# A decode step behind every half of the up phases, and one per two chunks in the down phases

## The reference, cut to what matters

```python
def _conv_ffn(x, buf, w_up, b_up, w_conv, b_conv, w_down):     # of the prompt, T = 2048
    h = jnp.einsum('btd,df->btf', x, w_up) + b_up               # D_MODEL 1024 -> 2 * D_FF, D_FF = 2816
    full = jnp.concatenate([buf.astype(h.dtype), h], axis=1)
    hc = b_conv + full[:, 0:T] * w_conv[0]
    for j in range(1, CONV_WIDTH):                              # CONV_WIDTH = 3
        hc = hc + full[:, j:j + T] * w_conv[j]
    gate, val = hc[..., :D_FF], hc[..., D_FF:]
    out = jnp.einsum('btf,fd->btd', jax.nn.gelu(gate) * val, w_down)
    ...
# of the decoded positions: q (8, 8, 8, 64), k_past and v_past (8, 8192, 8, 64) through page_table
s = jnp.einsum('bqhd,bkhd->bhqk', q, k) * ATTN_SCALE
s = s + qc[..., :, None] - kc[..., None, :]
p = jax.nn.softmax(jnp.where(causal, s, NEG_INF), axis=-1)
att = jnp.einsum('bhqk,bkhd->bqhd', p, v)
```

## Time and profile before

| what | value |
|---|---|
| median of three runs | 3660.61 us |
| the profiled execution's own time | 3655.41 us |
| its span | 3653.7 us |
| joint stage, PE's first to last matmul | 1459.8 to 3466.8, 2007 us |
| PE busy, whole span | 3179.5 us (87%) |
| DVE, ACT, POOL busy | 2090.3, 1744.2, 504.3 us |
| mean granted TensorE clock | 0.951 |

### The profile page before, as it was taken

One profiled execution on the slowest core, in us unless ns is written; L12 is line 12 of the kernel. 1 busy time (PEld: TensorE's weight loads), 2 busy tenths in 40 slices (PEclk: granted clock), 3 DMA queues, 4 the chain that ended last, 5 costly groups with the idle time before them and its releaser, 6 DMA issues. The chain is left out here.

```text
span 3653.7 us, 58230 instructions
## 1 busy us (share of the span) xinstructions
PE 3179.5 (87%) x20136; PEld 2513.4 (69%) x20136; DVE 2090.3 (57%) x3602; ACT 1744.2 (48%) x3497; POOL 504.3 (14%) x666
## 2 busy tenths in 40 slices
PE   6999943488888895999989999989999899999858
PEld 5999931377777684767767777667777677776623
DVE  2111155477777443666667666667666676665656
ACT  2111110366666311346645666446666456666445
POOL 0000000000000253001122111122111131112210
PEclk9999976799999997999999999999999999999979
DMA  4333333432320445657777766777666786757565
GB/s 142 111 115 105 114 119 142 116 74 67 81 60 1 136 152 157 208 173 253 258 242 282 266 224 237 270 266 269 216 244 231 263 288 239 252 196 250 199 264 212
DMA packets 313291, 684.44 MB, mean 187 GB/s; under 512 B 40151, under 2 KB 132215, under 8 KB 303999
## 3 DMA queue, kind: packets, MB, share of 16 engines
q1 hardware_dynamic: 264551, 519.21, 42.6%
q0 software_dynamic: 43840, 144.74, 11.4%
q10 hardware_dynamic: 4608, 16.78, 1.1%
HBM read 601.33 MB, written 79.92 MB: 186 GB/s over the span
## 5 line engine op out<-in xcount | busy, mean ns | idle before, releaser
L1705 DVE TENSOR_TENSOR F_w_lo<-F_raw,F_w_hi 128x512 fp32r<-128x512 f32 x704 | 500.0, 714 | 628.1 <-ACT F_w_hi L1601 626.9
L1601 ACT CAST F_w_hi<-F_raw 128x512 fp32r<-128x512 f32 x704 | 429.0, 614 | 438.5 <-DMA F_raw<-w_down 167.7
L1462 PE MATMUL F_ps_u<-F_x_hi,F_w_hi 128*128 128x512 f32 x1408 | 573.7, 407 | 27.9 <-DVE F_x_lo L1711 27.9
L1463 PE MATMUL F_ps_u<-F_x_lo,F_w_hi 128*128 128x512 f32 x1408 | 553.3, 393 | 0.0
L1464 PE MATMUL F_ps_u<-F_x_hi,F_w_lo 128*128 128x512 f32 x1408 | 552.2, 392 | 0.0
L1896 POOL DMA_DIRECT2D F_vin<-cache_v x512 | 280.6, 548 | 1482.9 <-PE F_ps_d L1529 1413.4
L1462 PEld LDWEIGHTS F_ps_u<-F_x_hi,F_w_hi 128*128 128x128 f32 x1408 | 266.7, 189 | 118.9 <-issue 53.3
L1462 PE MATMUL F_ps_y<-F_w_hi,F_g_hi 128*128 128x512 f32 x704 | 294.9, 419 | 57.2 <-DVE F_w_lo L1705 51.1
L1759 DVE STREAM_TRANSPOSE F_kt<-F_kin 128x1024 f32<-128x1024 f32 x256 | 303.7, 1222 | 39.0 <-PE F_ps_t L1518 23.1
L1464 PEld LDWEIGHTS F_ps_u<-F_x_hi,F_w_lo 128*128 128x128 f32 x1408 | 266.5, 189 | 58.0
L1463 PEld LDWEIGHTS F_ps_u<-F_x_lo,F_w_hi 128*128 128x128 f32 x1408 | 266.9, 190 | 48.5
(11 more groups left out here) (290 smaller groups left out, 5891.4 us busy)
## 6 DMA issues: line engine op xcount, KB each, us to landing
F_kin<-cache_k SPq DMA_DIRECT2D x512, 256.0 KB, 4.3
F_vin<-cache_v POOLq DMA_DIRECT2D x512, 256.0 KB, 4.6
F_raw<-w_up_t SPq DMA_DIRECT2D x176, 512.0 KB, 6.1
F_raw<-w_down SPq DMA_DIRECT2D x176, 512.0 KB, 5.7
S_raw<-w_up_t SPq DMA_DIRECT2D x22, 1024.0 KB, 10.3
sc_qk<-A_qk SPq DMA_DIRECT2D x16, 1024.0 KB, 5.7
S_raw<-w_down SPq DMA_DIRECT2D x11, 1024.0 KB, 9.9
A_prow<-w_in SPq DMA_DIRECT2D x8, 1028.0 KB, 4.9
```

The source lines that it names most:

```text
L1462: nc.tensor.matmul(out, a_hi, b_hi, start=first, stop=False)
L1463: nc.tensor.matmul(out, a_hi, b_lo, start=False, stop=False)
L1601: nc.scalar.copy(w_hi[:, q % 4, :], raw[:, unit % RAW, q % 2 * 512:(q % 2 + 1) * 512]).then_inc(hi_done, 1)
L1705: nc.vector.tensor_tensor(w_lo[:, q % 4, :], raw[:, q // 2 % RAW, q % 2 * 512:(q % 2 + 1) * 512], w_hi[:, q % 4, :].bitcast(F32), ALU.subt ...
```

## The change

One line, the rule that picks the halves with a place for a decode step. An up phase now has a place behind each of its 88 halves. A down phase has one at the second half of every second chunk (halves 0.5, 2.5, 4.5 and so on to 42.5), 22 in all. The number of places stays 88 + 22 = 110 for a block. The steps and their order are the same, and so is the work of each; they are dealt out to other halves. The last step comes at q = 677 instead of 685.

```diff
     def has_slot(q):
         i = q % HB
-        return i % 8 != 7 if i < UPH else (i - UPH) % 2 == 1 and (i - UPH) // 2 % 4 != 3
+        return i < UPH or (i - UPH) % 4 == 1
```

## The result

The change makes the kernel slower: 3694.50 us, median of four runs (3685.72 to 3700.56), against 3657.97 for the kernel before (3654.19 to 3662.54). The ratio is 1.0097, 95% interval 1.0073 to 1.0122, or +36.5 us. Forecast were 3649 us, in a range of 3630 to 3670. Rival (b), the QV steps that had filled waits, had 3677: the nearest, and still 17 us short.

A forecast was written before the change was run, and what follows sets the result against it. PE sets the pace and its work stays, so waits and the clock behind them were summed: -10.6 - 10.9 - 5 + 2 + 2 + 11.1 = -11.4 us, from a median of 3660.61 to 3649; range 3630 to 3670.

The forecast's parts named there:

- Rival (b): Down phases: QV at 9.5 and 21.5 had filled waits that other things set; +16.2 us, 3677, chance 0.13.
- Part 3: Down phases of blocks 0 to 2: 13.6 us of other, small waits fall by 5, between 0 and 10.
- Part 2: First sweep's end, halves 21.5 to 25.0 of blocks 0 to 2: 10.9 us less, bounds 0 and -14.
- Part 4: PE's wait near chunk 10 of the down phases, blocks 0 to 2 together: +2 us, between -4 and +8.
- The rest: Up phases of blocks 1 to 3: QV every 3 halves costs nothing while DVE's and ACT's lead lasts.
- waits that just move: Sign of a wrong prediction: the waits at the sweep's end only move instead of going away.
- Part 5: X groups behind sequences 1 and 3 move into up phases: 1 us a group, +2, between 0 and +5.
- Part 1: Sequence 0's steps Q and R, block 0's up phase: fewer waits for turned keys, -10.6 us, between -5 and -14.
- Part 6: Run of T and V at block 3's end of up phase: five waits of 1.94 us, +11.1, between +2.6 and +20.

The follow-up runs named there:

- e1: Changed kernel with its down-phase places shifted so that QV stands at halves 9.5, 21.5 and 41.5 in blocks 0 to 2: 3662.13 us.
- e12: Changed kernel with QV moved from 10.5 to 9.5 in the down phases of blocks 0 to 2, T left at 6.5: 3681.42 us.
- e8: Changed kernel with the last E and QV of its down phases at 39.5 and 41.5 instead of 38.5 and 40.5: 3687.99 us.
- e10: Kernel before, with QV moved from 9.5, 21.5 and 41.5 to 10.5, 22.5 and 40.5 in blocks 0 to 2: 3665.78 us.
- e2: Changed kernel with block 3 alone under the placement rule from before: 3678.97 us.
- e5: Changed kernel with the edits of e1 and e2 together: 3647.74 us.
- e4: Changed kernel with the next input's loads spread, one DMA at each of chunks 4, 6, 8 and 10: 3669.32 us.
- e11: Changed kernel with T moved from 6.5 to 5.5 in the down phases of blocks 0 to 2: 3687.47 us.
- e9: e5 with the X groups of blocks 0 and 2 two halves further on, two places there moved from up to down phase: 3640.31 us.

## Why the prediction was wrong, by its own steps

- **Part 3, other waits: wrong sign, and the largest error.** Forecast were 13.6 us falling by 5, outside of part 2's windows and chunk 10. They are 25.0 now (64.4 - 16.7 - 22.7): 11.4 us more. Of these 25.0, 14.3 are the new waits four chunks behind a T, and 6.3 are waits at the sweep's end that moved out of part 2's windows. The step took the waits as a cost that leaves with the steps and asked nowhere on which halves the steps that are left stand. e1 has the same number of steps in each phase with QV on its old halves, and there idle time is what I forecast.
- **Part 4, chunk 10: wrong in size.** +2 stood for three blocks. From half 6.0 to 11.0 they take 81.0 us against 75.1: +5.9, inside the bounds of -4 to +8. The step weighed one filler of 2.74 us against an earlier T. The filler is missing in full (7.42 - 4.74), and e12, which puts it back, is worth 13 us. The earlier T gives little. A QV at 5.5 stood ahead of T in block 2 alone, not in block 1, where the end of the wait lies as far behind half 6.0 as before (19.00 and 19.06 us); in block 2 it comes 1.2 us earlier (19.28 against 20.53).
- **"The rest": a term was missing.** The start of the up phases 1 to 3 was called unchanged, since their places are. But the last QV before them moved from 41.5 to 40.5, and the residual and T come 2.5 to 2.8 us later behind half 40.0 in all three. From half 41.0 to half 9 of the up phase, idle time is 13.0 us instead of 7.1 and the clock costs 7.3 us instead of nothing. e8, with QV at 41.5: 6.5 us. Rival (b) named 9.5 and 21.5, but not 41.5, and its mechanism, a wait with a fixed end, is not the one here.
- **Part 2, the first sweep's end: right in its window, partly by luck.** -10.9 forecast, -10.8 in the window. Over 20.0 to 28.0, with the waits that moved behind the window, idle time is 27.8 us before, 23.0 after, 24.8 in e1 and 21.8 in e10. So some of the gain is real, by QV's new place (e10) and by fewer steps (e1), and the sign of being wrong that I had named, waits that just move, holds for 6.3 of the 11.1 us.
- **Part 5, X groups: near its upper bound.** 1 us a group was taken from the earlier trace rows, a row with QV at the other kind of half. The groups at `i % 4 == 0` wait 2.1 to 2.6 each, 9.2 in four; with what the groups waited before, the up phases have 4.8 us more, +2 forecast, 0 to +5 the bounds.
- **Part 1, sequence 0: two thirds of it.** The two waits of 2.62 are gone, as forecast, but PE waits 7.4 us for keys, not 4: won 3.8 instead of 7.2. The clock gave back 3.3 us up to half 32, where 3.4 were forecast (5.7 to 2.4 in this pair of profiles; other runs with the same steps there have 8.2 and 9.0 before, 2.5 to 4.4 after).
- **Part 6, T and V run: right.** Five waits of 1.94 us, 9.7 us more idle time in the stretch (+11.1 forecast with the clock, which did not fall behind each). e2: 15.5 us for all of block 3. The drain of about 1380 ns behind a table load (the Trainium skill, "ScalarE: Activation LUTs", What ACT_TABLE_LOAD costs) is not seen here either: in the chain ahead of the wait at 3348.98, gelu starts 1.29 us after its load does (3344.78 to 3346.07) and exp 1.30 us after its own (3346.72 to 3348.02).

So the step that failed is parts 3 and 4 together with the rest: -3 us were forecast for them, and the profiles show +11.4 of idle time, +5.9 us, and +5.9 of idle time with 7.3 of clock. The three repairs made singly, e2 (15.5), e12 (13) and e8 (6.5), sum to 35 of the 36.5 us; they were not run together, and e8's share is not clear of the noise. e1 and e2 together (e5) more than undo the loss. Rival (b) said of chunk 10 what e12 and the fixed end of that wait confirm, at a chance of 0.13; I put it low because I judged it by the sweep's end, the one place where it indeed does not hold. How the clock's part divides over the causes stays open, and so does the cause of the new waits behind T.

## What to carry to other kernels

Before filler work is moved, list each long wait of the bounding engine with what ends it, and note which fillers stand in front of it. If that end doesn't depend on the engine's own progress (a DMA behind other DMAs, for instance), a filler moved from in front to behind costs its whole length. Then follow what hangs on the filler, its loads and its work on the other engines: these move too, and can move the end of a wait, as at the start of the up phases. A count of places per phase says little by itself; here the same count gave 3694 and 3662 us, and with the tail and the X groups put right as well 3640. Where the chain behind the wait is long enough to hold the engine for several steps on end, look at the whole stretch: a window that ends within it can show a gain that has only moved.

## What the runs showed of the hardware

A long wait of PE is paid twice, but the second part is smaller than its record suggests. The low clock begins while PE still waits: at the wait of 7.42 us 0.50 (1.2 GHz) holds for 10.2 us, of which PE is busy for some 5, so that about 2.5 us are lost on top; at the wait of 4.02 us 6.8 us, of which some 5.4 busy, so 2.7. Cut in pieces, the same idle time can leave the clock alone: in e8 1.21, 1.05 and 1.58 us within 22 us left it at 1.00. That held in every profile of these schedules: from half 41.0 to half 9 of the next up phase the three blocks lost 4.8 to 7.3 us of clock in the kernel after, e2, e4, e11 and e12, with one wait of 2.8 to 4.2 us at T and 11.0 to 15.7 us of idle time in all, and nothing in the kernel before, e1 and e8, with 7.1 to 11.2 us of idle time in short waits. The five waits of 1.94 us had one low stretch of 3.4 us among them, less than the earlier trace rows made me expect. The sum of these losses scatters from run to run: blocks 0 to 2 with the same steps lost 35.0 us in one profile (the kernel after) and 27.9 in another (e2). Of the joint stage's sums, 40.1 us after, 26.0 before and 20.9 in e9, the first and last differ by more than that.
